# Seven block products in place of eight for the gate and up projections, with the block sums on VectorE

## Chip, core and metric

The kernel runs on one core of a Trainium2 chip. The metric is the device time of one execution in microseconds; lower is better. TensorE (PE; PEld are its weight loads) multiplies, VectorE (DVE) and ScalarE (ACT) do the elementwise work, SyncE (SP) issues the weight transfers from HBM. All arithmetic is f32.

## What is computed

Three transformer layers over 256 latent tokens (`x`) and 256 context tokens (`ctx`) of width 1024. Layer 0 has two kinds of attention and a feed-forward over both token sets, layer 1 has latent attention (MLA) and a feed-forward over the latent tokens alone, layer 2 has a gated linear recurrence, a gating unit and 16 experts. The change concerns the two feed-forwards (`ffn_w13` is 1024 x 5632, `ffn_w2` 2816 x 1024 per layer):

```python
def swiglu(h, w13, w2):
    gate, up = jnp.split(h @ w13, 2, axis=-1)
    return (jax.nn.silu(gate) * up) @ w2

# layer l, after attention (layer 0 does the same for ctx):
hx = modulate(rmsnorm(x, norm_g[l, 2]), mx[:, 3], mx[:, 4])
x = x + mx[:, 5] * rmsnorm(swiglu(hx, ffn_w13[l], ffn_w2[l]), norm_g[l, 3])
```

## The kernel before

Activations lie transposed in SBUF: `H[:, k, :]` holds channels 128k to 128k+127 of 512 tokens, the latent tokens in columns 0:256, the context in 256:512. A projection of 128 output columns is one accumulation over k = 0..7: stationary operand a 128x128 block of weights, moving operand `H[:, k, :]` (256 or 512 columns), output one of seven PSUM banks that are used in turn (`take`, `pe_dense`; L350 in `mm` issues every matmul).

Weights come through `ring`, six slots of 128x4096 f32 (2 MB), in the fixed order of `jobs`: job j goes to slot j % 6. SP issues them one after another and waits, before job j, until `weights_used` shows that job j-6 was read. A job `("w13", l, i)` holds 256 gate columns (0:256 of each k) and the 256 up columns that belong to them (256:512), so two pairs of 128; eleven such jobs, then eight jobs of `ffn_w2`.

First feed-forward (`pe_ffn0`, `act_ffn0`, `dve_ffn0`): the projections of jobs 0 and 1 run apart for the latent and the context half (256 columns each), because the context half is normalised later. Jobs 2 to 10, 18 pairs, run as gate and up with 512 columns: 16 matmuls a pair. ScalarE takes Silu of the gate product out of PSUM into `TG` (L935), VectorE multiplies by the up product into `HID` (L960) and so frees the bank. After the last of these, PE starts on `ffn_w2` with the same 512 tokens.

Second feed-forward (`pe_ffn1`, `act_ffn1`, `dve_ffn1`): the same over the 256 latent tokens, all 22 pairs alike, 16 matmuls of 256 columns each; Silu at L989, multiply at L998.

Every instruction of VectorE and ScalarE waits for the end of the one before on its own engine (`Chain.step`, `mark`, `free`); `full_of` waits for a PSUM bank to be full, `freed` for it to be empty again.

Of the kernel before, what the change touches and what calls it, by code (L numbers as in the profile page):

```python
# [23 lines left out]
P = 128  # L24
# [124 lines left out]
def build(nc, A, tab_f, tab_m, vrows, out):  # L149
    es = ExitStack()  # L150
    with es:
# [95 lines left out]
        logf_ready = Signal(sem("logf_ready"))  # L247


        jobs, job_at = [], {}  # L250

        def job(label, *dmas):
            job_at[label] = len(jobs)
            jobs.append(dmas)
# [37 lines left out]
        for i in range(2):  # L292
            job(("ab_out", i), rows(A["ab_w_out"][0], 0, D, i * 512, (i + 1) * 512))
        ffn_jobs(0)
# [34 lines left out]
        for j, dmas in enumerate(jobs):  # L329
            loads[j % SLOTS] += len(dmas)  # L330
            loaded_at.append(16 * loads[j % SLOTS])
# [26 lines left out]
        def weights(pe, label):  # L358
            j = job_at[label]
            pe.wait_ge(slot_loaded[j % SLOTS], loaded_at[j])  # L360
            return ring[:, j % SLOTS, :]
# [510 lines left out]

        HID = ar(0, KF, T2)
# [7 lines left out]
        def pe_ffn0(pe):  # L881
# [13 lines left out]
            for i in range(2, NW):  # L895
                w = w13(pe, 0, i)
                for j in range(2):
                    for g in range(2):
                        pe_dense(pe, ("gu"[g], 0, 2 * i + j), w, 256 * g + j * P, H, T2)
                used()  # L900
            freed(pe, ("u", 0, KF - 1))
# [14 lines left out]
        def act_ffn0(c):  # L916
# [15 lines left out]
            for j in range(4, KF):  # L932
                b = full_of(c.eng, ("g", 0, j))
                freed(c.eng, ("u", 0, j - 2) if j >= 6 else ("u", 0, j - 2, 1))
                c.free(S.activation(TG[:, j % 2, :], ps[:, b, :], ACT.Silu), ("g", 0, j))  # L935
# [13 lines left out]
        def dve_ffn0(c):  # L949
            for j in range(4):  # L950
# [4 lines left out]
            for j in range(KF):  # L955
                key, t = (("u", 0, j, 1), HALF[1]) if j < 4 else (("u", 0, j), slice(0, T2))
                freed(c.eng, ("g",) + key[1:])
                b = full_of(c.eng, key)
                src = ps[:, b, 0:TX] if j < 4 else ps[:, b, :]
                c.free(V.tensor_tensor(HID[:, j, t], TG[:, j % 2, t], src, ALU.mult), key)  # L960
# [10 lines left out]
        def pe_ffn1(pe):  # L971
            for i in range(NW):
# [5 lines left out]
            freed(pe, ("u", 1, KF - 1))  # L978
# [5 lines left out]
        def act_ffn1(c):  # L984
            for j in range(KF):
                b = full_of(c.eng, ("g", 1, j))
                if j >= 2:
                    freed(c.eng, ("u", 1, j - 2))
# [1312 lines left out]
```

## Time and profile before

| | |
|---|---|
| median of 3 runs | 2561.03 us (2557.65 to 2563.27) |
| the profiled execution | 2562.76 us |
| its span, first to last instruction | 2561.0 us |
| PE busy / PEld / DVE / ACT | 2096.5 / 1200.3 / 547.2 / 422.1 us |
| gate/up projections, first feed-forward (whole width) | from about 460 to 707 us |
| gate/up projections, second feed-forward | 1054.6 to 1210.4 us |
| experts | from about 1623 us to the end |

The page gives one profiled execution. An f32 matmul shows as two records of PE and two of PEld. The chain of waits names, from the end backwards, what each piece waited for; the share of an engine in it is the part of the time that it set.

### The profile page before, as it was taken

The numbers are of one execution on the slowest core, as the hardware profiler recorded it, in microseconds if no ns is written. First come the engines' busy times: TensorE is split into PE (matmuls) and PEld (weight loads), VectorE is DVE, ScalarE is ACT, GpSimd is POOL, SyncE is SP. The second block draws the span as 40 slices with busy tenths as digits, with TensorE's granted clock in tenths as the row PEclk, the third lists the DMA queues.
The fourth block names the chain that finished last, engine by engine and source line by source line (L and its number), as shares of the span: only waits on it lengthen the run. The fifth ranks groups of instructions, "written<-read, shape, count | busy, mean of one in ns | idle before, by whom it ended". The sixth has DMA issues, their size and how long they took to land.

```text
span 2561.0 us, 25876 instructions
## 1 busy us (share of the span) xinstructions
PE 2096.5 (82%) x10863; PEld 1200.3 (47%) x10863; DVE 547.2 (21%) x1203; ACT 422.1 (16%) x883; POOL 7.0 (0%) x15
## 2 busy tenths in 40 slices
PE   6998899999999999999999999755565656555555
PEld 3544368544446857888887777411111111111111
DVE  3217744000000456300026622200000000000001
ACT  3005534000000446300033221100000000000000
POOL 0000000000000000000000000000000000000000
PEclk9999999999999999999999989877778777778777
DMA  9447862221122440444532323699999999999996
GB/s 381 189 197 309 309 204 69 96 87 47 46 74 56 118 146 8 132 149 110 187 126 99 131 76 140 277 428 428 428 427 428 427 427 428 427 428 428 428 427 282
DMA packets 178498, 614.77 MB, mean 240 GB/s; under 512 B 26096, under 2 KB 119536, under 8 KB 144592
## 3 DMA queue, kind: packets, MB, share of 16 engines
q1 hardware_dynamic: 177568, 610.38, 60.9%
q0 software_dynamic: 816, 2.76, 0.4%
q8 instruction: 86, 1.41, 0.2%
q14 instruction: 28, 0.23, 0.0%
HBM read 612.06 MB, written 1.05 MB: 239 GB/s over the span
## 4 chain that ended last, share of the span: by engine, by line
PE 60%; DMA 33%; DVE 4%; ACT 1%; issue 1%; SPq 0%; DVEq 0%; ACTq 0%
PE ps L350 58%; DMA ring<-in_expert_w_up 13%; DMA ring<-in_expert_w_gate 11%; DMA ring<-in_expert_w_down 8%; DMA ring<-in_ab_w_in 1%; PE ps L762 1%; DVE ST L797 0%; DVE X L709 0%; DVE AR L708 0%; ACT AR L815 0%; ACT AR L827 0%; DVE H L660 0%; PE ps L491 0%; DVE AR L849 0%; PE ps L2019 0%
## 5 line engine op out<-in xcount | busy, mean ns | idle before, releaser
L350 PE MATMUL ps<-ring,AR 128*32 128x512 f32 (+1 forms) x4096 | 516.1, 651 | 359.8 <-DMA ring<-in_expert_w_up 128.9
L350 PE MATMUL ps<-H,ring 128*128 128x256 f32 (+1 forms) x2848 | 795.2, 441 | 8.2 <-ACT H L646 4.9
L350 PEld LDWEIGHTS ps<-H,ring 128*128 128x128 f32 x2848 | 542.8, 191 | 251.0 <-issue 193.2
L350 PEld LDWEIGHTS ps<-ring,AR 128*32 128x32 f32 x4096 | 143.0, 132 | 713.5 <-issue 241.2
L350 PE MATMUL ps<-AR,ring 128*128 128x256 f32 (+1 forms) x1228 | 316.7, 420 | 2.5 <-DVE AR L1788 1.0
L350 PEld LDWEIGHTS ps<-AR,ring 128*128 128x128 f32 x1228 | 234.6, 191 | 83.6 <-issue 53.1
L350 PE MATMUL ps<-AR 128*128 128x128 f32 (+5 forms) x848 | 129.9, 356 | 19.2 <-ACT AR L815 8.6
L2053 DVE TENSOR_TENSOR AR<-AR,ps 128x512 f32<-128x512 f32 x16 | 11.0, 687 | 581.1 <-PE ps L350 581.1
L350 PEld LDWEIGHTS ps<-AR 128*128 128x128 f32 (+2 forms) x848 | 88.4, 183 | 47.3 <-issue 38.4
L2039 ACT ACTIVATE AR<-ps 128x512 f32<-128x512 f32 x16 | 9.6, 597 | 535.5 <-PE ps L350 535.5
L2064 DVE TENSOR_TENSOR AR<-ps,X 32x256 f32<-32x256 f32 x64 | 26.9, 420 | 286.2 <-PE ps L350 284.5
L350 PE MATMUL ps<-ring,H 128*128 128x512 f32 (+1 forms) x224 | 76.6, 502 | 0.0
L350 PE MATMUL ps<-ring,SC 128*32 128x512 f32 x576 | 68.7, 602 | 2.5 <-DMA ring<-in_ada_w 2.5
L960 DVE TENSOR_TENSOR AR<-AR,ps 128x512 f32<-128x512 f32 (+1 forms) x22 | 14.1, 639 | 260.6 <-PE ps L350 260.6
L797 DVE TENSOR_REDUCE ST<-ps 128x1 f32<-128x512 f32 (+1 forms) x96 | 57.8, 602 | 25.9 <-PE ps L350 23.8
L815 ACT ACTIVATE AR<-ps,ST 128x512 f32<-128x512 f32 (+1 forms) x96 | 59.2, 617 | 24.1 <-DVE ST L804 20.9
L2045 ACT ACTIVATE AR<-ps 128x512 f32<-128x512 f32 x16 | 9.6, 597 | 319.3 <-PE ps L2019 319.3
L350 PEld LDWEIGHTS ps<-ring,H 128*128 128x128 f32 x224 | 37.5, 191 | 37.8 <-issue 37.7
L703 DVE TENSOR_TENSOR H<-H 128x256 f32<-128x256 f32 x21 | 8.9, 426 | 200.9 <-ACT H L689 200.8
L762 PEld LDWEIGHTS ps<-FTAB,AR 128*128 128x128 f32 x272 | 30.3, 143 | 42.7 <-issue 38.8
L762 PE MATMUL ps<-FTAB,AR 128*128 128x128 f32 x272 | 41.2, 284 | 10.3 <-DVE AR L849 7.2
L935 ACT ACTIVATE AR<-ps 128x512 f32<-128x512 f32 x18 | 10.8, 598 | 233.2 <-PE ps L350 233.2
(255 smaller groups left out, 1086.8 us busy)
## 6 DMA issues: line engine op xcount, KB each, us to landing
ring<-in_expert_w_gate SPq DMA_DIRECT2D x64, 2048.0 KB, 23.3
ring<-in_expert_w_up SPq DMA_DIRECT2D x64, 2048.0 KB, 23.3
ring<-in_expert_w_down SPq DMA_DIRECT2D x64, 2048.0 KB, 23.1
ring<-in_ada_w SPq DMA_DIRECT2D x36, 2048.0 KB, 10.1
ring<-in_ffn_w SPq DMA_DIRECT2D x44, 1024.0 KB, 7.6
ring<-in_w_in SPq DMA_DIRECT2D x12, 2048.0 KB, 7.9
ring<-in_ffn_w SPq DMA_DIRECT2D x16, 1408.0 KB, 7.1
ring<-in_ab_w_in SPq DMA_DIRECT2D x4, 2048.0 KB, 15.9
```

The lines of the kernel that those rows point to most:

```text
L350: m = nc.tensor.matmul(out_, lhsT=lhsT, rhs=rhs, start=start, stop=stop)
L703: ins = V.tensor_tensor(self.SQ(0)[:, self.t], self.SQ(0)[:, self.t], self.SQ(k)[:, self.t], ALU.add)
L762: m = nc.tensor.transpose(ps[:, b, j * P:(j + 1) * P], PR[:, i % 2, u, j * P:(j + 1) * P], ident)
L797: c.step(V.reduce_max(st[:, m:m + 1], ps[:, b, 0:g.nk], axis=AX_X))
L815: c.free(S.activation(PR[:, i % 2, m, 0:g.nk], ps[:, b, 0:g.nk], ACT.Exp, bias=st[:, 2 + m:3 + m], scale=g.scale, accum_out=st[:, 6 + m:7 ...
L935: c.free(S.activation(TG[:, j % 2, :], ps[:, b, :], ACT.Silu), ("g", 0, j))
L960: c.free(V.tensor_tensor(HID[:, j, t], TG[:, j % 2, t], src, ALU.mult), key)
L2039: c.free(S.activation(GT, ps[:, b, :], ACT.Silu), ("hg", e))
L2045: c.free(S.activation(HT.rearrange("p a b -> p (a b)"), ps[:, b, :], ACT.Copy), ("ht", e))
L2053: c.free(V.tensor_tensor(HS, GT, ps[:, b, :], ALU.mult), ("hu", e))
L2064: ins = V.tensor_tensor(YE[32 * q:32 * q + 32, g, t * TX:(t + 1) * TX], ps[32 * t:32 * t + 32, b, 0:TX], GFR[32 * t:32 * t + 32, t, :], AL ...
```

## The change

The product of each pair and all its tokens is seen as two by two blocks: the weights as gate and up (128 columns each) by lower and upper half of the 1024 channels, `A11, A12` (gate) and `A21, A22` (up); the activations as halves of the channels by halves of the tokens, `B11, B12, B21, B22` (first feed-forward: latent and context, 256 each; second: 128 and 128 latent tokens). Eight block products of four matmuls each become seven (Strassen's scheme in Winograd's form), with half as many columns per matmul: 28 matmuls of 256 columns in the first feed-forward in place of 16 of 512, 28 of 128 in the second in place of 16 of 256.

The new class `Pairs` has this work: `dve_four` makes the four sums of activations once per feed-forward; `dve_blocks` the four sums of weights for each pair (one of them in place, in the ring); PE runs the products 1, 2, 6, 7, 5, 4, 3; ScalarE copies product 1 out of PSUM and takes both Silus from SBUF; VectorE adds the other products together (seven adds) and does two multiplies by the Silus. PE waits for the block sums of a pair ahead of product 6. The sums of the next pair stand in VectorE's order after product 5.

Jobs 2 to 10 of the first feed-forward and 1 to 10 of the second are done so: 18 and 20 pairs. The four sums of activations of the first feed-forward lie in the ring slot of `ab_out` 1, which is kept until the last `w13` job was read; so each job now notes its own slot and the job that it has to wait for. The diff, with the parts that only rename left out:

```diff
@@ -245,12 +245,20 @@
         logf_ready = Signal(sem("logf_ready"))
         jobs, job_at = [], {}
+        slot_of, after, last_in = [], [], [s - SLOTS for s in range(SLOTS)]
         def job(label, *dmas):
-            job_at[label] = len(jobs)
+            s = min(range(SLOTS), key=lambda a: last_in[a])
+            slot_of.append(s)
+            after.append(int(last_in[s]))
+            last_in[s] = job_at[label] = len(jobs)
             jobs.append(dmas)
@@ -291,6 +299,8 @@
             job(("ab_out", i), rows(A["ab_w_out"][0], 0, D, i * 512, (i + 1) * 512))
+        held_slot = slot_of[job_at[("ab_out", 1)]]
+        last_in[held_slot] = len(jobs) + KF // 2 - 0.5
         ffn_jobs(0)
@@ -870,6 +880,120 @@
+        class Pairs:
+            def __init__(self, l, i0, T, H_, HID_, sums, four, C, V_, W):
+                self.l, self.T, self.HID, self.sums, self.four, self.C, self.V, self.W = l, T, HID_, sums, four, C, V_, W
+                self.at = [(i, j) for i in range(i0, NW) for j in range(2)]
+                self.x, self.y = slice(0, T), slice(T, 2 * T)
+                self.low, self.high = (H_[:, 4 * a:4 * a + 4, :] for a in range(2))
+                n = len(self.at)
+                self.four_base = four_ready.plan(1)
+                self.block_base = blocks_ready.plan(n)
+                self.silu = silu_ready.plan(2 * n)
+                self.hid = pair_hid.plan(2 * n)
+            def block(self, p, m, a):
+                i, j = self.at[p]
+                n = job_at[("w13", self.l, i)]
+                w = ring[:, slot_of[n], :].rearrange("p (k n) -> p k n", k=KD)
+                return w[:, 4 * a:4 * a + 4, 256 * m + j * P:256 * m + (j + 1) * P]
+            def pe(self, pe):
+                T1, T2, T3, T4 = self.four
+                (B11, _), (B21, B22) = ((h[:, :, self.x], h[:, :, self.y]) for h in (self.low, self.high))
+                for p, (i, j) in enumerate(self.at):
+                    if j == 0:
+                        w13(pe, self.l, i)
+                    S1, S2, S4 = self.sums[p % 2]
+                    A11, A12, S3, A22 = (self.block(p, m, a) for m in range(2) for a in range(2))
+                    for n, A_, B_ in ((1, A11, B11), (2, A12, B21), (6, S2, T2), (7, S3, T3), (5, S1, T1), (4, A22, T4),
+                                      (3, S4, B22)):
+                        b = take(pe, ("p", n, self.l, p))
+                        if n == 6:
+                            if p == 0:
+                                pe.wait_ge(four_ready.sem, self.four_base + 1)
+                            pe.wait_ge(blocks_ready.sem, self.block_base + p + 1)
+                        for k in range(4):
+                            mm(ps[:, b, 0:self.T], A_[:, k, :], B_[:, k, :], k == 0, k == 3, b if k == 3 else None)
+                    if j:
+                        used()
+            def act(self, c):
+                for p in range(len(self.at)):
+                    v, w = self.C[p % 2], self.V[p % 2]
+                    b = full_of(c.eng, ("p", 1, self.l, p))
+                    c.free(S.activation(v, ps[:, b, 0:self.T], ACT.Copy), ("p", 1, self.l, p))
+                    if p >= 2:
+                        c.eng.wait_ge(pair_hid.sem, self.hid + 2 * (p - 1))
+                    freed(c.eng, ("p", 2, self.l, p))
+                    c.mark(S.activation(TG[:, p % 2, self.x], v, ACT.Silu), silu_ready, self.silu + 2 * p + 1)
+                    freed(c.eng, ("p", 3, self.l, p))
+                    c.mark(S.activation(TG[:, p % 2, self.y], w, ACT.Silu), silu_ready, self.silu + 2 * p + 2)
+            def dve_four(self, c):
+                T1, T2, T3, T4 = self.four
+                (B11, B12), (B21, B22) = ((h[:, :, self.x], h[:, :, self.y]) for h in (self.low, self.high))
+                c.step(V.tensor_tensor(T1, B12, B11, ALU.subtract))
+                c.step(V.tensor_tensor(T2, B22, T1, ALU.subtract))
+                c.step(V.tensor_tensor(T3, B22, B12, ALU.subtract))
+                c.mark(V.tensor_tensor(T4, B21, T2, ALU.subtract), four_ready, self.four_base + 1)
+            def dve_blocks(self, c, p):
+                S1, S2, S4 = self.sums[p % 2]
+                A11, A12, A21, A22 = (self.block(p, m, a) for m in range(2) for a in range(2))
+                n = job_at[("w13", self.l, self.at[p][0])]
+                c.eng.wait_ge(slot_loaded[slot_of[n]], loaded_at[n])
+                c.step(V.tensor_tensor(S1, A21, A22, ALU.add))
+                c.step(V.tensor_tensor(A21, A11, A21, ALU.subtract))
+                c.step(V.tensor_tensor(S2, S1, A11, ALU.subtract))
+                c.mark(V.tensor_tensor(S4, A12, S2, ALU.subtract), blocks_ready, self.block_base + p + 1)
+            def hid_of(self, p, t):
+                i, j = self.at[p]
+                return self.HID[:, 2 * i + j, t]
+            def dve_gated(self, c, p, half, src):
+                c.eng.wait_ge(silu_ready.sem, self.silu + 2 * p + half + 1)
+                t = (self.x, self.y)[half]
+                c.mark(V.tensor_tensor(self.hid_of(p, t), src, TG[:, p % 2, t], ALU.mult), pair_hid,
+                       self.hid + 2 * p + half + 1)
+            def dve(self, c):
+                last = len(self.at) - 1
+                def product(p, n):
+                    return ps[:, full_of(c.eng, ("p", n, self.l, p)), 0:self.T]
+                self.dve_blocks(c, 0)
+                for p in range(last + 1):
+                    v, u, w = self.C[p % 2], self.V[p % 2], self.W
+                    y = self.hid_of(p, self.y)
+                    freed(c.eng, ("p", 1, self.l, p))
+                    p6 = product(p, 6)
+                    c.free(V.tensor_tensor(u, v, p6, ALU.add), ("p", 6, self.l, p))
+                    p2 = product(p, 2)
+                    c.free(V.tensor_tensor(v, v, p2, ALU.add), ("p", 2, self.l, p))
+                    if p:
+                        self.dve_gated(c, p - 1, 1, self.hid_of(p - 1, self.y))
+                    p7 = product(p, 7)
+                    c.free(V.tensor_tensor(w, u, p7, ALU.add), ("p", 7, self.l, p))
+                    p5 = product(p, 5)
+                    c.step(V.tensor_tensor(y, w, p5, ALU.add))
+                    c.free(V.tensor_tensor(u, u, p5, ALU.add), ("p", 5, self.l, p))
+                    if p < last:
+                        self.dve_blocks(c, p + 1)
+                    p4 = product(p, 4)
+                    c.free(V.tensor_tensor(w, w, p4, ALU.add), ("p", 4, self.l, p))
+                    self.dve_gated(c, p, 0, w)
+                    p3 = product(p, 3)
+                    c.free(V.tensor_tensor(u, u, p3, ALU.add), ("p", 3, self.l, p))
+                self.dve_gated(c, last, 1, self.hid_of(last, self.y))
         HID = ar(0, KF, T2)
@@ -892,13 +1016,8 @@
                     used()
-            for i in range(2, NW):
-                w = w13(pe, 0, i)
-                for j in range(2):
-                    for g in range(2):
-                        pe_dense(pe, ("gu"[g], 0, 2 * i + j), w, 256 * g + j * P, H, T2)
-                used()
-            freed(pe, ("u", 0, KF - 1))
+            pairs0.pe(pe)
+            pe.wait_ge(pair_hid.sem, pairs0.hid + 2 * len(pairs0.at))
@@ -929,10 +1048,9 @@
                     c.free(S.activation(TG[:, j % 2, HALF[part]], ps[:, b, 0:TX], ACT.Silu), ("g", 0, j, part))
-            for j in range(4, KF):
-                b = full_of(c.eng, ("g", 0, j))
-                freed(c.eng, ("u", 0, j - 2) if j >= 6 else ("u", 0, j - 2, 1))
-                c.free(S.activation(TG[:, j % 2, :], ps[:, b, :], ACT.Silu), ("g", 0, j))
+            for j in (2, 3):
+                freed(c.eng, ("u", 0, j, 1))
+            pairs0.act(c)
             smooth_table()
@@ -947,17 +1065,25 @@
         def dve_ffn0(c):
+            def first_hid(c, j):
+                key = ("u", 0, j, 1)
+                freed(c.eng, ("g",) + key[1:])
+                b = full_of(c.eng, key)
+                c.free(V.tensor_tensor(HID[:, j, HALF[1]], TG[:, j % 2, HALF[1]], ps[:, b, 0:TX], ALU.mult), key)
             for j in range(4):
...
                 c.mark(V.tensor_tensor(hid, hid, TG[:, j % 2, HALF[0]], ALU.mult), hid_ready, j + 1)
-            for j in range(KF):
-                key, t = (("u", 0, j, 1), HALF[1]) if j < 4 else (("u", 0, j), slice(0, T2))
-                freed(c.eng, ("g",) + key[1:])
-                b = full_of(c.eng, key)
-                src = ps[:, b, 0:TX] if j < 4 else ps[:, b, :]
-                c.free(V.tensor_tensor(HID[:, j, t], TG[:, j % 2, t], src, ALU.mult), key)
+            for j in range(2):
+                first_hid(c, j)
+            c.eng.wait_ge(weights_used, job_at[("ab_out", 1)] + 1)
+            for k in range(KD):
+                pre0f[1].ready(c.eng, k)
+            pairs0.dve_four(c)
+            for j in range(2, 4):
+                first_hid(c, j)
+            pairs0.dve(c)
             for k in range(1, SPLIT):
@@ -969,33 +1095,41 @@
         def pe_ffn1(pe):
-            for i in range(NW):
+            for i in range(1):
                 w = w13(pe, 1, i)
...
                 used()
-            freed(pe, ("u", 1, KF - 1))
+            pairs1.pe(pe)
+            pe.wait_ge(pair_hid.sem, pairs1.hid + 2 * len(pairs1.at))
+            for j in range(2):
+                freed(pe, ("u", 1, j))
             for n in range(KD):
...
         def act_ffn1(c):
-            for j in range(KF):
+            for j in range(2):
                 b = full_of(c.eng, ("g", 1, j))
-                if j >= 2:
-                    freed(c.eng, ("u", 1, j - 2))
                 c.free(S.activation(TG[:, j % 2, 0:TX], ps[:, b, 0:TX], ACT.Silu), ("g", 1, j))
+            for j in range(2):
+                freed(c.eng, ("u", 1, j))
+            pairs1.act(c)
             smooth_table()
...
         def dve_ffn1(c):
-            for j in range(KF):
+            for k in range(KD):
+                pre1f.ready(c.eng, k)
+            pairs1.dve_four(c)
+            for j in range(2):
                 freed(c.eng, ("g", 1, j))
...
                 c.free(V.tensor_tensor(HID1[:, j, :], TG[:, j % 2, 0:TX], ps[:, b, 0:TX], ALU.mult), ("u", 1, j))
+            pairs1.dve(c)
             for k in range(1, KD):
@@ -2102,6 +2236,13 @@
         yf = ar(11264, KD, T2)
+        def block_sums(at):
+            return [[ar(at + 1536 * q + 512 * a, 4, P) for a in range(3)] for q in range(2)]
+        pairs0 = Pairs(0, 2, TX, H, HID, block_sums(12288),
+                       [ring[:, held_slot, 1024 * a:1024 * (a + 1)].rearrange("p (k t) -> p k t", k=4) for a in range(4)],
+                       [RS[:, q * TX:(q + 1) * TX] for q in range(2)],
+                       [FREED[:, q * TX:(q + 1) * TX] for q in range(2)], FREED[:, 2 * TX:3 * TX])
         post0f = [PartPost(("ffn", 0), 0, 1, p, lambda k: yf[:, k, :], lambda k: H[:, k, :], SPLIT) for p in range(2)]
@@ -2111,6 +2252,8 @@
         yg = ar(5632, KD, TX)
+        pairs1 = Pairs(1, 1, P, H[:, :, HALF[0]], HID1, block_sums(8192), [ar(13312 + 512 * a, 4, P) for a in range(4)],
+                       [FREED[:, q * P:(q + 1) * P] for q in range(2)], [FREED[:, q * P:(q + 1) * P] for q in (2, 3)], FREED[:, 4 * P:5 * P])
         post1f = PartPost(("ffn", 1), 1, 1, 0, lambda k: yg[:, k, :], lambda k: H[:, k, :])
@@ -2179,11 +2322,11 @@
             for j, dmas in enumerate(jobs):
-                s = j % SLOTS
+                s = slot_of[j]
                 if j == 4:
                     sp.dma_start(FTAB[:, FT_FIRST:FT_W], tab_f[:, FT_FIRST:FT_W]).then_inc(tables_loaded, 16)
-                if j >= SLOTS:
-                    sp.wait_ge(weights_used, j - SLOTS + 1)
+                if after[j] >= 0:
+                    sp.wait_ge(weights_used, after[j] + 1)
                 for dst, src in dmas:
```

## Rows read from the trace of the kernel before

**Rows 1.** The page: slices of the span (GB/s), and the chain by engine, by line.

```profile
GB/s 381 189 197 309 309 204 69 96 87 47 46 74 56 118 146 8 132 149 110 187 126 99 131 76 140 277 428 428 428 427 428 427 427 428 427 428 428 428 427 282
...
PE 60%; DMA 33%; DVE 4%; ACT 1%; issue 1%; SPq 0%; DVEq 0%; ACTq 0%
```

**Rows 2.** Busy time by stretch: window and length, PE, PEld, DVE, ACT, POOL, clock, DMA, GB/s.

```profile
117.85:125.00 7.15, 7.15 (x66) 7.15 (x65) 4.03 (x7) 0.83 (x3) 0.00 (x0) 1.00 0.98 409
...
500.00:550.00 50.00, 50.00 (x118) 22.23 (x117) 2.75 (x4) 2.39 (x4) 0.00 (x0) 1.00 0.26 84
...
1100.00:1150.00 50.00, 50.00 (x233) 44.03 (x232) 2.95 (x7) 2.69 (x7) 0.00 (x0) 1.00 0.50 155
```

**Rows 3.** The waits of SP's queue: us in total, times, longest.

```profile
SPq L2188 <- PE ps L350: 2334.6, 287, 67.8
```

**Rows 4.** Timeline of DVE, first feed-forward: start, duration, instruction, idle time before it.

```profile
500.73 0.69 DVE L960 TENSOR_TENSOR AR<-AR,ps 128x512 f32<-128x512 f32 x1 [13.05 <-PE ps L350]
...
555.67 0.69 DVE L960 TENSOR_TENSOR AR<-AR,ps 128x512 f32<-128x512 f32 x1 [13.05 <-PE ps L350]
```

**Rows 5.** The same, where the first feed-forward has 256 columns (context half).

```profile
438.81 0.42 DVE L960 TENSOR_TENSOR AR<-AR,ps 128x256 f32<-128x256 f32 x1 [6.06 <-PE ps L350]
...
459.53 0.42 DVE L960 TENSOR_TENSOR AR<-AR,ps 128x256 f32<-128x256 f32 x1 [6.48 <-PE ps L350]
```

**Rows 6.** Timeline of ACT in the value projection of layer 0 (128 columns).

```profile
119.90 0.28 ACT L1062 ACTIVATE AR<-ps 128x128 f32<-128x128 f32 x1 [12.69 <-PE ps L350]
...
125.26 0.28 ACT L1062 ACTIVATE AR<-ps 128x128 f32<-128x128 f32 x1 [1.51 <-PE ps L350]
```

**Rows 7.** Groups of DVE by line and form: count, busy us, mean ns, idle before.

```profile
L1617 DVE TENSOR_TENSOR H<-AR 128x512 f32<-128x512 f32 x16 | 11.1, 692 | 0.5
...
L855 DVE COPY H<-ps 128x128 f32<-128x128 f32 x32 | 9.3, 292 | 6.9 <-PE ps L350 5.9
...
L1640 DVE TENSOR_TENSOR H<-AR 128x1024 f32<-128x1024 f32 x4 | 4.9, 1226 | 6.7 <-ACT AR L1600 6.7
```

**Rows 8.** Timeline of a normalisation, DVE and ACT in turn.

```profile
379.79 0.42 DVE L708 TENSOR_TENSOR AR<-AR,RS 128x256 f32<-128x256 f32 x1 [3.98 <-ACT RS L584]
380.24 0.42 DVE L709 TENSOR_TENSOR X<-X,AR 128x256 f32<-128x256 f32 x1
...
380.76 0.42 ACT L639 ACTIVATE H<-X 128x256 f32<-128x256 f32 x1 [1.06 <-DVE X L709]
...
393.52 0.42 ACT L584 ACTIVATE RS<-RS 128x256 f32<-128x256 f32 x1
394.05 4.13 DVE L666 SCALAR_TENSOR_TENSOR H<-X,AMP,RS 128x256 f32<-128x256 f32 x8 [3.62 <-ACT RS L584]
```

**Rows 9.** Groups of ACT by line and form.

```profile
L1062 ACT ACTIVATE AR<-ps 128x128 f32<-128x128 f32 x4 | 1.1, 278 | 17.2 <-PE ps L350 17.2
...
L639 ACT ACTIVATE H<-X 128x256 f32<-128x256 f32 x56 | 23.4, 417 | 33.4 <-DVE X L709 29.7 <-DVE X L565 2.8
...
L989 ACT ACTIVATE AR<-ps 128x256 f32<-128x256 f32 x22 | 8.4, 384 | 135.7 <-PE ps L350 135.7
```

**Rows 10.** Timeline where the second feed-forward goes over to ffn_w2.

```profile
1209.94 0.42 DVE L998 TENSOR_TENSOR AR<-AR,ps 128x256 f32<-128x256 f32 x1 [6.48 <-PE ps L350]
...
1210.41 4.80 PE L350 MATMUL ps<-AR,ring 128*128 128x256 f32 x21 [0.61 <-DVE AR L998]
```

**Rows 11.** The page's DMA issues: KB each, us to landing.

```profile
ring<-in_ffn_w SPq DMA_DIRECT2D x44, 1024.0 KB, 7.6
```

**Rows 12.** Groups by form: weight loads of the projections.

```profile
L350 PEld LDWEIGHTS ps<-H,ring 128*128 128x128 f32 x2816 | 537.6, 191 | 249.3 <-issue 193.2 <-ACT H L607 1.8 <-ACT H L646 1.0
```

**Rows 13.** Busy time and clock, columns as in rows 2.

```profile
280.00:300.00 20.00, 15.99 (x122) 7.04 (x122) 12.47 (x37) 10.80 (x29) 0.00 (x0) 1.00 0.79 300
...
1052.00:1056.00 4.00, 1.65 (x5) 1.00 (x4) 2.45 (x6) 2.81 (x7) 0.00 (x0) 0.73 0.00 0
```

More of the change, by code:

```diff
@@ L247, in build @@
         logf_ready = Signal(sem("logf_ready"))
+        four_ready = Signal(sem("four_ready"))
+        blocks_ready = Signal(sem("blocks_ready"))
+        silu_ready = Signal(sem("silu_ready"))
+        pair_hid = Signal(sem("pair_hid"))
         jobs, job_at = [], {}
+        slot_of, after, last_in = [], [], [s - SLOTS for s in range(SLOTS)]
         def job(label, *dmas):
-            job_at[label] = len(jobs)
+            s = min(range(SLOTS), key=lambda a: last_in[a])
+            slot_of.append(s)
+            after.append(int(last_in[s]))
+            last_in[s] = job_at[label] = len(jobs)
             jobs.append(dmas)
@@ L329, in build @@
         for j, dmas in enumerate(jobs):
-            loads[j % SLOTS] += len(dmas)
-            loaded_at.append(16 * loads[j % SLOTS])
+            loads[slot_of[j]] += len(dmas)
+            loaded_at.append(16 * loads[slot_of[j]])
         place, takes = {}, [0] * BANKS
@@ L359, in weights @@
             j = job_at[label]
-            pe.wait_ge(slot_loaded[j % SLOTS], loaded_at[j])
-            return ring[:, j % SLOTS, :]
+            pe.wait_ge(slot_loaded[slot_of[j]], loaded_at[j])
+            return ring[:, slot_of[j], :]
         def used():
```

## Prediction

> **What bounds the kernel now.** I read the page's chain of waits first, then the busy time by stage, then single stretches of the timeline. The chain is 60% TensorE and 33% DMA [rows 1]. The DMA part is the expert stage: from slice 26 on the transfers run at 427 to 428 GB/s [rows 1]. Both stretches that the change touches are TensorE's alone. In the first feed-forward's gate/up stage PE is busy 50.00 of 50 us at granted clock 1.00, DVE 2.75 and DMA 26%; in the second PE is again 50.00 of 50, DVE 2.95, DMA 50% [rows 2]. So TensorE time saved there shortens the path one for one, until another engine becomes late. The weight queue is no clock of its own: SP waited 2334.6 us for PE in 287 waits [rows 3]; slots are released by matmuls, so when PE is early the expert transfers start earlier by the same amount, with unchanged length.
>
> **TensorE's price of the products.** A pair (gate and up of 128 columns) is 16 matmuls of 512 columns in the first feed-forward. The same pass of VectorE over its result comes every (555.67 - 500.73)/4 = 13.735 us [rows 4]. At 256 columns, 16 matmuls take (459.53 - 438.81)/3 = 6.907 us [rows 5], 0.4317 each, in groups of eight with no extra per group. After the change a pair is 7 products of 4 matmuls: 28 x 0.4317 = 12.09 us. Saved: 1.65 us a pair, 18 pairs, **29.7 us**.
> In the second feed-forward a pair is 16 matmuls of 256 columns, 6.905 us; after it is 28 of 128 columns. The nearest row is the 32 matmuls of 128 columns in the value projection, shown as 64 records, two to a matmul, where ScalarE's evictions after each eight matmuls are (125.26 - 119.90)/3 = 1.787 us apart [rows 6]: 0.2233 each (a little more than half of 0.4317), so 28 x 0.2233 = 6.25 us. TensorE alone would save 0.65 x 20 = 13.1 us.
>
> **What VectorE gets.** Per pair: seven adds that read a product, two gate multiplies, four block sums of 128x512. Prices: 692 ns for 128x512 (also where, as in L1617, the operands are strided halves), 292 for 128x128, 1226 for 128x1024 [rows 7], 425 for 128x256 [rows 5, 8]; a dependent instruction follows about 0.03 us after the end of the one before, and a hand-over from VectorE to ScalarE or back costs 0.10 us [rows 8]. ScalarE: 0.38 to 0.42 at 256 columns; at 128 columns 0.278 from PSUM, and I estimate 0.31 from SBUF, by the same 0.03 that separate the two at 256 [rows 9]. PE's end to VectorE is 0.14 us, VectorE to PE 0.05 [rows 10].
> First feed-forward: 9 x 0.455 + 4 x 0.722 = 7.0 us a pair, with the one hop over ScalarE (0.10 + 0.42 + 0.03 + 0.38 + 0.10, less the gap counted) 8.0, against 12.09 of PE. It is covered with 4 us to spare. The new wait of PE for the sums sits before the third product; behind it in PE's queue are all later matmuls. The sums of the next pair are made after product 5 is read: 0.14 + 0.91 + 2.89 = 3.9 us against the four products (6.9 us) that PE has left. Free.
> Second feed-forward: here nothing is left over. The loop that VectorE and ScalarE must go round per pair, with no matmul in it: after the sums, add of product 4, gate multiply, add of product 3 (3 x 0.322 = 0.97); ScalarE's Silu of the second half and only behind it its copy of the next pair's product 1, since it takes them in that order (0.10 + 0.31 + 0.03 + 0.28 + 0.10, less 0.03, = 0.79); adds of 6 and 2, gate multiply, adds of 7 and twice 5 (6 x 0.322 = 1.93); four sums (2.89). Together **6.58, say 6.6 us**, against 6.25 of TensorE and 6.905 before. The loop through PE (sums ready, products 6, 7, 5, then adds and sums: 0.05 + 2.68 + 0.14 + 0.64 + 2.89 = 6.4) is a little shorter. So VectorE's chain sets the pace and PE idles 0.35 us in each pair: half of the saving there is lost.
>
> **The ends of the stages.** First feed-forward, start: VectorE must do four sums of 128x1024 (4 x 1.26 = 5.0 us) between the context products of columns 1 and 2, which come 6.9 us apart [rows 5]: hidden. The sums of pair 0 wait behind the last of these gate multiplies, 0.14 + 0.45 + 2.89 = 3.5 us after its matmuls, while PE has products 1 and 2 (3.45 us): 0.1 us. End: before, PE waited for one pass (0.14 + 0.69 + 0.05 = 0.88); now product 3, add, Silu, multiply: 0.14 + 0.42 + 0.10 + 0.42 + 0.10 + 0.42 + 0.05 = 1.65. So the first feed-forward gains 29.7 - 0.1 - 0.8 = **28.8 us**.
> Second: the first block (four projections as before) is unchanged, and the four sums of 128x512 made before its first eviction lie under its 13.8 us of matmuls. Then the sums of pair 0 end 3.5 us after its last matmul; 19 rounds of 6.6 follow; the last pair ends 5.8 us after its sums (four more products and the Silu tail, same prices). 3.5 + 125.4 + 5.8 = 134.7, against 20 x 6.905 + 0.61 [rows 10] = 138.7 before. **4.0 us** gained.
> The ring keeps one slot back for the four sums of the first feed-forward, so prefetch goes five deep in place of six. A two-part weight job lands in about 8 us [rows 11] and is used for 24.2; its cover is four jobs, some 97 us. Nothing on SP's queue comes later than it is needed. VectorE's own wait for the next job's weights is covered by the same lead; were it late, the adds of products 4 and 3 behind it would hold two PSUM banks that PE wants a pair later.
> Sum: 28.8 + 4.0 = 32.8. The profiled execution took 2562.8 us (span 2561.0), so 2530.0; the median of the runs shown is 1.7 lower, and I put the forecast at **2529**. All stages behind shift unchanged; re-warming of TensorE's clock at the gaps behind may move it by some 2 us.
>
> **Rivals.**
> A. ScalarE's hop or VectorE's small adds are cheaper and the second feed-forward is TensorE-bound: 19 x 0.35 = 6.6 us more, 2522. For it: only 0.35 us a pair separate the two. Against: every term comes from a row, and all VectorE instructions are dependent.
> B. The same chain is longer: instructions of 0.29 us with two or three waits each may follow less tightly than the 0.42 us ones of [rows 8], and a PE that restarts after a gap has to load weights first. At 7.1 us a pair the second feed-forward loses 5.5 us against before: 2539.
> C. Slower than before: the stationary loads bound the 128-column stream. In the value projection PEld was busy 7.15 of 7.15 us [rows 2], and a load shows 191 ns, two to a matmul, where 256 columns cover it [rows 12]. If long streams paid that in full, a matmul would take 0.382, a pair 28 x 0.382 = 10.7 us, 20 pairs 76 us more, and the whole 2563 - 28.8 + 76 = 2610. It decides from 6.905 + 28.8/20 = 8.3 us a pair, 0.298 per matmul. Against: those 32 matmuls ran at 0.2233 with a new load for each [rows 6].
> The Trainium skill, page "TensorE: Matmul & The Clock Gate", section "Back-to-back issue gap", speaks for C in a milder form: it gives about 81 ns for each load-and-matmul pair of 128 columns in a sustained stream. Taking our f32 matmul as four such passes that would be an estimate of 0.324, 9.07 us a pair, and 2577 in all. The row of 0.2233 disagrees, and I go by the row.
> D. The idle 0.35 us per pair lowers the granted clock. It fell to 0.73 where PE was busy only 1.65 of 4 us, but it stayed at 1.00 with 15.99 of 20 busy in many small gaps [rows 13]. At half clock a pair would need 12 us: about 2640. Little speaks for it.
> E. The gain is made and given back: a weight transfer becomes the late one behind. With the queue idle as in [rows 2, 3], I see no place; up to 2560.
>
> **How the numbers follow.** Forecast 0.60 (2525 to 2533), A 0.15, B 0.15 (up to 2545), C 0.04, D 0.02, E 0.04. A range from 2519 (A, less the 1.7 us and the clock's 2) to 2540 (B at 7.1 us) leaves out C, D, E and the end of B. About 0.2% (5 us) is what a measurement of this kernel can tell from no change. Faster by more: forecast, A, B and most of E, 0.93; within: 0.02; slower: C and D, with a little for what I don't see, 0.05.
>
> **What would show it.** Right: in the first feed-forward TensorE 100% busy at clock 1.00 and pairs 12.1 us apart, VectorE near 7 us of each; in the second, pairs 6.6 us apart, VectorE about 90% busy, PE waiting some 0.3 us a pair for the last block sum, loads all but continuous. The expert stage has its old length. Wrong: pairs at 6.25 (A) or above 6.9 (B) in the second, matmuls of 128 columns slower than 0.23 us while no wait is shown (C), a granted clock below 1.00 there (D), or waits of PE for in_ffn_w, mla or in2 transfers (E).

## Result and the profile after

The changed kernel takes 2530.04 us (median of 4 runs, 2527.80 to 2534.51) against 2561.35 before (median of 4, 2557.65 to 2563.27): a ratio of 0.9882, 95% interval 0.9870 to 0.9895, so 31.3 us less. The profiled execution took 2527.8 us, its span is 2525.8.

The page of the changed kernel: busy time, and the chain by engine, which answer to [rows 1].

```profile
PE 2053.2 (81%) x11775; PEld 1285.2 (51%) x11775; DVE 759.7 (30%) x1667; ACT 443.5 (18%) x959; POOL 7.0 (0%) x15
...
PE 57%; DMA 33%; DVE 7%; ACT 2%; issue 1%; SPq 0%; DVEq 0%; ACTq 0%
```

The chain is the chain of waits that ended last. PE's part of it fell from 60 to 57%, and DVE's rose from 4 to 7%: it now runs over VectorE somewhere. Busy time by stretch of the changed kernel (columns as in [rows 2]) says where:

```profile
500.00:550.00 50.00, 50.00 (x234) 44.01 (x233) 27.14 (x54) 5.29 (x13) 0.00 (x0) 1.00 0.27 85
1100.00:1150.00 50.00, 48.62 (x423) 47.49 (x423) 40.52 (x99) 6.60 (x22) 0.00 (x0) 1.00 0.40 112
```

In the first feed-forward PE is still busy all the time. In the second it is not, and VectorE is busy 40.52 of 50 us, at an unchanged clock of 1.00.

The span cut at the same five instructions in both traces (first matmul of the attention output; first of `ffn_w2`; first of the second feed-forward; first of its `ffn_w2`; first of the experts):

| stage, us | before | after | difference |
|---|---|---|---|
| up to the attention output | 347.00 | 344.73 | -2.27 |
| attention output, gate/up of the first feed-forward | 360.48 | 331.97 | **-28.51** |
| `ffn_w2` and MLA | 347.12 | 347.68 | +0.56 |
| gate/up of the second feed-forward | 155.81 | 153.33 | **-2.48** |
| rest up to the experts | 408.65 | 406.48 | -2.17 |
| experts | 941.94 | 941.61 | -0.33 |

The two changed stages give 31.0 of the 35.2 us by which the two profiled spans differ; the rest is stages that the change does not touch. Over the profiles of all kernels below, the first stage lies between 344.7 and 349.4 us and the one up to the experts between 406.5 and 409.2, while the 331.97 comes again to 0.01 us in each kernel that leaves that stage alone. A stage's length therefore tells more here than a median. The second feed-forward's is less steady: without any change to it one kernel below had 154.50 where the kernel before had 155.81. The difference lies in its first 32 matmuls, which are the same in all kernels but start at a granted clock of 0.50 for longer or shorter: until about 1060.3 us in the kernel before, 5.7 us into the stage, until about 1029 in the changed one, 4.6 us into it. So that stage is best cut in two, behind these 32 matmuls (busy time by stretch; the kernel before first, then the changed one):

```profile
1054.60:1071.50 16.90, 16.90 (x64) 14.18 (x65) 3.14 (x7) 5.88 (x11) 0.00 (x0) 0.82 0.40 125
1071.50:1210.41 138.91, 138.30 (x641) 121.41 (x639) 8.84 (x21) 8.96 (x21) 0.00 (x0) 1.00 0.43 128
```

```profile
1024.38:1040.59 16.21, 16.21 (x64) 13.71 (x65) 5.91 (x11) 5.88 (x11) 0.00 (x0) 0.86 0.40 129
1040.59:1177.71 137.12, 129.95 (x1122) 126.53 (x1120) 108.02 (x261) 18.41 (x61) 0.00 (x0) 1.00 0.44 130
```

Of the 2.48 us the change gives 138.91 - 137.12 = 1.8; the other 0.7 us is the clock at the stage's start (a mean of 0.86 in place of 0.82). The stretch of the changed pairs, from that cut to `ffn_w2`, is called the pair stretch below.

The first feed-forward after, timeline of VectorE: the same add of two successive pairs, to be held against [rows 4].

```profile
550.87 0.42 DVE L985 TENSOR_TENSOR AR<-FTAB,ps 128x256 f32<-128x256 f32 x1 [1.30 <-PE ps L360]
...
562.96 0.42 DVE L985 TENSOR_TENSOR AR<-FTAB,ps 128x256 f32<-128x256 f32 x1 [1.30 <-PE ps L360]
```

12.09 us apart, where it was 13.735. VectorE waits 1.30 us for PE here: it has room.

The second, as the chain of waits goes through one pair (start, length, what; the short pieces of "issue" between VectorE's instructions are left out):

```profile
1090.33 0.70 DVE AR L953
1091.04 0.14 issue
1091.17 2.93 PE ps L360 x24
1094.10 0.03 issue
1094.13 0.02 DVEq L379
1094.15 0.04 issue
1094.19 0.30 DVE AR L985
...
1094.52 0.30 DVE FTAB L986
...
1094.84 0.70 DVE AR L950
...
1095.57 0.70 DVE ring L951
...
1096.29 0.70 DVE AR L952
...
1097.02 0.70 DVE AR L953
1097.72 0.14 issue
1097.86 2.25 PE ps L360 x18
```

L953 is the last block sum. PE starts 0.14 us behind it, does products 6, 7 and 5 (24 records, 12 matmuls, 2.93 us), VectorE takes product 5 at 1094.19 in two adds and makes the four sums. From 1091.17 to 1097.86 are **6.69 us a pair**: less than the 6.905 of before, more than the 6.25 of TensorE alone. This is a loop through two engines: PE cannot start product 6 before VectorE's sums, and VectorE makes the next sums only behind product 5.

The four places where the stages begin and end, timeline of PE (in square brackets the idle time before):

```profile
460.74 1.53 PE L360 MATMUL ps<-ring,AR 128*128 128x256 f32 x6 [0.15 <-DVE AR L953]
...
676.70 1.55 PE L360 MATMUL ps<-AR,ring 128*128 128x512 f32 x3 [1.62 <-DVE AR L962]
...
1044.37 1.13 PE L360 MATMUL ps<-AR 128*128 128x128 f32 x8 [1.83 <-DVE AR L953]
...
1177.71 1.56 PE L360 MATMUL ps<-AR,ring 128*128 128x256 f32 x6 [1.25 <-DVE AR L962]
```

### The profile page after: what moved, and what is told of

The parts are those of the page before. It is cut to its first block, busy times and chain, and to the rows that moved or that the text cites. A ratio compares the mean times of both kernels' runs of the same rounds, so it can differ in the third digit from the quotient of the medians.

```text
span 2525.8 us, 28670 instructions
## 1 busy us (share of the span) xinstructions
PE 2053.2 (81%) x11775; PEld 1285.2 (51%) x11775; DVE 759.7 (30%) x1667; ACT 443.5 (18%) x959; POOL 7.0 (0%) x15
## 4 chain that ended last, share of the span: by engine, by line
PE 57%; DMA 33%; DVE 7%; ACT 2%; issue 1%; SPq 0%; DVEq 0%; ACTq 0%
PE ps L360 55%; DMA ring<-in_expert_w_up 14%; DMA ring<-in_expert_w_gate 9%; DMA ring<-in_expert_w_down 8%; PE ps L772 1%; DMA ring<-in_ada_w 1%; DVE AR L950 1%; DVE AR L953 1%; DVE AR L952 1%; DVE ring L951 1%; DVE ST L807 0%; DVE AR L718 0%; DVE X L719 0%; ACT AR L825 0%; ACT AR L837 0%
## 5 line engine op out<-in xcount | busy, mean ns | idle before, releaser
L360 PE MATMUL ps<-ring,AR 128*32 128x256 f32 (+2 forms) x4384 | 581.6, 631 | 360.6 <-DMA ring<-in_expert_w_up 133.5
L360 PEld LDWEIGHTS ps<-ring,AR 128*32 128x32 f32 (+1 forms) x4384 | 197.1, 135 | 719.5 <-issue 246.0
L360 PE MATMUL ps<-H,ring 128*128 128x256 f32 (+2 forms) x2240 | 513.5, 388 | 7.6 <-ACT H L656 5.1
L360 PEld LDWEIGHTS ps<-H,ring 128*128 128x128 f32 x2240 | 403.9, 192 | 103.8 <-issue 55.0
L360 PE MATMUL ps<-AR,ring 128*128 128x256 f32 (+2 forms) x1548 | 358.5, 389 | 3.9 <-DVE AR L962 2.9
L360 PEld LDWEIGHTS ps<-AR,ring 128*128 128x128 f32 x1548 | 273.3, 191 | 84.3 <-issue 53.1
L360 PE MATMUL ps<-AR 128*128 128x128 f32 (+5 forms) x1168 | 171.3, 332 | 25.2 <-ACT AR L825 8.6
L360 PE MATMUL ps<-ring 128*128 128x256 f32 x288 | 68.0, 379 | 0.0
L360 PE MATMUL ps<-H,AR 128*128 128x128 f32 (+2 forms) x320 | 60.5, 333 | 2.4 <-ACT H L617 2.4
L360 PEld LDWEIGHTS ps<-ring 128*128 128x128 f32 x288 | 54.7, 190 | 7.4
```

The source lines that it names most:

```text
L360: m = nc.tensor.matmul(out_, lhsT=lhsT, rhs=rhs, start=start, stop=stop)
```

## Experiments

**Which loop sets the second feed-forward.** The theory on record is VectorE's chain with ScalarE's hop: VectorE waits for ScalarE's copy of product 1, and ScalarE copies only behind a Silu that waits for VectorE. The trace after, where VectorE waits 0.09 us for product 5, speaks for the loop through PE. Two orders can be changed without changing any work.

`act_early`, ScalarE's copy of the next product 1 ahead of its second Silu (`copy` holds the two lines that stood at the head of the loop):

```diff
...
+                    if p + 1 < len(self.at):
+                        copy(p + 1)
                     freed(c.eng, ("p", 3, self.l, p))
                     c.mark(S.activation(TG[:, p % 2, self.y], w, ACT.Silu), silu_ready, self.silu + 2 * p + 2)
```

> ScalarE copies the next pair's product 1 before it takes the Silu of this pair's second half; nothing else moves. The changed kernel's pairs in the second feed-forward are 6.69 us apart. Theory on record (the chain of VectorE with ScalarE's hop in it sets the pace): the hop of 0.79 us leaves the chain, pairs come 6.4 us apart or less, 19 x 0.3 = 5.5 us or more gained. Rival, read off the trace after (the loop through the stopped PE sets it: sums ready, PE restarts 0.15 us later, three products 2.92, 0.10, two adds, four sums): pairs stay at 6.69 us, total within 1 us of the changed kernel, and VectorE's wait ahead of the add of product 5 grows from 0.1 us to some 0.9.

Timeline of VectorE and PE:

```profile
1091.51 0.29 DVE L990 TENSOR_TENSOR AR<-FTAB,ps 128x128 f32<-128x128 f32 x1 [0.49 <-PE ps L360]
...
1095.18 1.13 PE L360 MATMUL ps<-AR 128*128 128x128 f32 x8 [0.20 <-DVE AR L958]
...
1098.20 0.29 DVE L990 TENSOR_TENSOR AR<-FTAB,ps 128x128 f32<-128x128 f32 x1 [0.49 <-PE ps L360]
```

Pairs stay at 6.69 us. The hop is gone from VectorE's chain, and all that it bought is that VectorE waits longer for PE: 0.49 us for product 5, not the 0.9 expected there; another 0.44 comes ahead of the add of product 6. The time was 2533.85 us (0.9890, 0.9875 to 0.9905), nominally more than the changed kernel's; the pair stretch took 137.06 us (137.12 in the changed kernel), and the surplus lies in the first stage (349.4) and the one up to the experts (409.1).

`blocks_early`, the sums of the next pair ahead of the adds of product 5:

```diff
...
+                    if p < last:
+                        self.dve_blocks(c, p + 1)
                     p5 = product(p, 5)
                     c.step(V.tensor_tensor(y, w, p5, ALU.add))
                     c.free(V.tensor_tensor(u, u, p5, ALU.add), ("p", 5, self.l, p))
-                    if p < last:
-                        self.dve_blocks(c, p + 1)
```

> The four block sums of the next pair are made ahead of the two adds of product 5 and not behind them; ScalarE's order is as in the changed kernel. Loop through PE sets the pace: it gets 1.5 us shorter, and then the chain of VectorE with ScalarE's hop is what is left: pairs at 6.60 us, 19 x 0.09 = 1.7 us gained. Theory on record (that chain sets the pace already): it contains the same instructions in either order, so 6.69 us stays, 0 gained. If neither were a bound: 6.25.

Its timeline of VectorE: the first add behind the sums, and the add that waits for ScalarE's copy.

```profile
1092.14 0.29 DVE L987 TENSOR_TENSOR AR<-FTAB,ps 128x128 f32<-128x128 f32 x1
...
1094.53 0.29 DVE L977 TENSOR_TENSOR FTAB<-FTAB,ps 128x128 f32<-128x128 f32 x1 [0.80 <-ACT FTAB L928]
...
1098.74 0.29 DVE L987 TENSOR_TENSOR AR<-FTAB,ps 128x128 f32<-128x128 f32 x1
```

6.60 us: with the loop through PE shortened, the chain that the prediction had worked out is left, at its forecast length, with VectorE idle in it only for the hop. The median, 2530.00 (0.9874), shows no gain, but the trace does: the pair stretch took 134.12 us, 3.0 less. 1.7 of it are 19 x 0.09; the rest lies in the first pairs behind pair 0, where PE waits for no sums yet (three of them follow at 6.25 to 6.33 us).

`both_early`, the two together:

> Both moves. Each theory has both loops shorter than the products themselves: VectorE needs 9 x 0.322 + 4 x 0.722 = 5.8 us a pair. Then TensorE is the bound, 28 x 0.2233 = 6.25 us a pair, 19 x 0.44 = 8.4 us less than the changed kernel. If the 128-column matmul costs more in a long stream than in the 32 matmuls of the value projection (loads become the bound), pairs would be longer than 6.25 with PE never waiting.

2521.44 us (0.9843, 0.9828 to 0.9858), with a pair stretch of 128.53 us. Timeline of VectorE, the add of product 6:

```profile
1092.51 0.29 DVE L982 TENSOR_TENSOR FTAB<-FTAB,ps 128x128 f32<-128x128 f32 x1 [0.46 <-PE ps L360]
...
1098.77 0.29 DVE L982 TENSOR_TENSOR FTAB<-FTAB,ps 128x128 f32<-128x128 f32 x1 [0.46 <-PE ps L360]
```

The pairs are 6.26 us apart. In the pair stretch the two moves alone give 0.1 and 3.0 us, and neither shows in a median; together they give 8.6 us, in the pair stretch and in the median alike.

`all_early`, both moves, and the block sums of pair 0 one gate multiply earlier in both feed-forwards (shown for the second):

```diff
...
             for j in range(2):
+                if j:
+                    pairs1.dve_blocks(c, 0)
                 freed(c.eng, ("g", 1, j))
```

> As both_early, and the block sums of pair 0 ahead of the last gate multiply of the part before, in both feed-forwards. The changed kernel has PE idle 1.83 us there in the second and 0.15 us in the first. Expected: 1.9 us less than both_early, so some 10 us less than the changed kernel. If a bank or a transfer were late instead, no gain over both_early.

2519.00 us (2517.41 to 2519.35), ratio 0.9832 (0.9815 to 0.9848), the fastest of those that do no needless work; stages 331.58 and 142.41 us, 0.4 and 1.7 less than with both moves. Busy time by stretch:

```profile
1100.00:1150.00 50.00, 50.00 (x450) 50.00 (x449) 42.98 (x104) 7.17 (x24) 0.00 (x0) 1.00 0.44 117
```

PE and its loads are busy without a gap, at full clock.

**Each part alone.** `first_only` has the second feed-forward of before, `second_only` the first.

> Seven products in the first feed-forward alone; the second as in the kernel before. Prediction's sum: 28.8 us less than before (2532.5). By the traces of before and after the stage is 28.5 us shorter and nothing is given back, so 28 to 29 less. If the freed time were lost behind (a weight transfer late), less than 25.

> Seven products in the second feed-forward alone, first one and ring as before. Prediction's sum 4.0 us less than before; the trace after shows the stage 2.5 us shorter (pairs at 6.69 in place of 6.60). So 2.5 less, near the limit of what can be measured. If the parts act on each other, the two do not add up to 31.

`first_only` took 2532.90 us (0.9888, 0.9873 to 0.9902; 28.5 less than the 2561.4 beside it), stage 331.97: the first feed-forward is nearly everything. `second_only` took 2556.99 us (0.9985, 0.9976 to 0.9995; 4.4 less, with an interval of 1.3 to 6.1), pairs at 6.69 us: the second feed-forward is a small gain. Its trace puts it lower than the median does: 136.81 us for the pair stretch, 2.1 less than before. 28.5 and 4.4 add up to 32.9 against 31.3 measured together, within the intervals: no run shows the two acting on each other.

**What a block sum costs in the loop, and beside it.** The same sum made again, once a pair in the second feed-forward (below); four times, or three, with `self.l == 0` for the first:

```diff
...
+                if self.l == 1:
+                    for _ in range(1):
+                        c.step(V.tensor_tensor(S1, A21, A22, ALU.add))
                 c.step(V.tensor_tensor(S1, A21, A22, ALU.add))
```

> The changed kernel with one block sum per pair made twice, in the second feed-forward only (19 of them in the loop). If VectorE's instructions lie on the loop that sets the pace, each costs its whole 0.72 us: pairs at 7.41 us, total 14 us more. If PE set the pace and VectorE were only busy beside it, up to 0.44 us of it would be hidden.

2546.51 us, 16.5 more than the changed kernel. Timeline of VectorE, an add of product 5 in successive pairs:

```profile
1104.03 0.29 DVE L988 TENSOR_TENSOR AR<-FTAB,ps 128x128 f32<-128x128 f32 x1
...
1111.44 0.29 DVE L988 TENSOR_TENSOR AR<-FTAB,ps 128x128 f32<-128x128 f32 x1
```

Pairs are 7.41 us apart, 6.69 + 0.72: every sum costs its whole length there. The expected 14 us left out two things: the sum of pair 0 (0.7 us), and the clock behind the longer wait for it, seen in the timeline of PE and in busy time by stretch:

```profile
1047.38 1.61 PE L360 MATMUL ps<-AR 128*128 128x128 f32 x8 [2.55 <-DVE AR L956]
```

```profile
1047.40:1050.50 3.10, 3.10 (x17) 3.10 (x18) 0.58 (x2) 0.31 (x1) 0.00 (x0) 0.57 1.10 350
```

Pair 1 starts 9.04 us behind pair 0 there and not 7.41: 1.6 us more.

> The changed kernel with four more block sums per pair in the first feed-forward only (18 x 2.9 = 52 us more of VectorE work). Forecast: VectorE has 4 us to spare per pair and the sums 3.0 us ahead of their use, so the pairs stay 12.09 us apart and only pair 0 pays its 2.9 us (sums of pair 0 are not hidden): 3 us more in all. If VectorE shared a bound with PE there: up to 52 us.

This expectation failed: 2540.58 us, 10.5 more, and the stage was 341.22 us, 9.25 more. Timeline of PE, two starts of product 6 after a block sum:

```profile
567.11 1.97 PE L360 MATMUL ps<-ring,AR 128*128 128x256 f32 x8
...
579.47 1.97 PE L360 MATMUL ps<-ring,AR 128*128 128x256 f32 x8
```

12.36 us apart: a new bound, and by the same loop as in the second feed-forward. Twelve matmuls of 256 columns 5.18, two adds 0.91, eight sums 5.79; 0.48 is left for PE's stop, restart and hand-over. In the second feed-forward 6.69 - 2.68 - 0.65 - 2.89 = 0.47 is left. I had again allowed 0.14 on one side and nothing on the other. Of the 9.25 us, 17 x 0.27 = 4.6 are this, 2.9 the sums of pair 0, and the rest, 1.8, the clock behind their wait. Timeline of PE, and the granted clock (last but two):

```profile
466.55 2.98 PE L360 MATMUL ps<-ring,AR 128*128 128x256 f32 x8 [3.06 <-DVE AR L956]
...
469.32 2.60 PE L360 MATMUL ps<-ring 128*128 128x256 f32 x8
...
471.76 1.89 PE L360 MATMUL ps<-ring,AR 128*128 128x256 f32 x8
```

```profile
466.50:469.00 2.50, 2.45 (x8) 2.05 (x9) 0.00 (x0) 0.00 (x0) 0.00 (x0) 0.67 0.62 194
469.00:472.00 3.00, 3.00 (x12) 2.49 (x11) 0.84 (x2) 0.42 (x1) 0.00 (x0) 0.71 0.00 0
```

After 3.06 us of idleness two products took 5.21 us in place of 3.45: 0.67 and 0.71 are means of stretches at 1.00 and at 0.50, and by slices of 1 us the clock was 0.50 from 467.5 to 470.5. Two more runs test the loop:

> The changed kernel with three more block sums per pair in the first feed-forward (four gave 12.36 us a pair). If the loop sums, PE's restart, three products, two adds, sums sets that 12.36, one sum less gives 11.64, below the 12.09 of the products: pairs at 12.09 again, and only the sums of pair 0 cost their 2.2 us more, perhaps with a window of lower clock behind that wait. If VectorE's work slowed PE in proportion: 12.3.

> The version with everything early (sums of the next pair ahead of the adds of product 5, ScalarE's copy first, sums of pair 0 one multiply earlier), with the same four extra sums per pair in the first feed-forward that gave 12.36 us a pair. Loop theory: the loop now holds two products and one add, 12.36 - 1.73 - 0.46 = 10.2; VectorE needs 4.1 + 8 x 0.722 = 9.9. So the products bound: 12.09 a pair and no cost beyond pair 0's. If four extra sums cost by themselves (memory shared with PE): again 12.3 or more.

With three extra sums, timeline of PE (product 6 of two successive pairs):

```profile
572.20 1.89 PE L360 MATMUL ps<-ring,AR 128*128 128x256 f32 x8
...
584.28 1.89 PE L360 MATMUL ps<-ring,AR 128*128 128x256 f32 x8
```

12.08 us, and the stage is 2.18 us longer than the changed kernel's, its pair 0 alone; 2532.17 us. With four, but early, busy time by stretch:

```profile
500.00:550.00 50.00, 50.00 (x234) 44.01 (x233) 37.98 (x70) 4.86 (x12) 0.00 (x0) 1.00 0.27 84
```

VectorE is busy 76% of the time, PE is not slowed at all: stage 331.58 us, the same as without the extra sums, 2518.09 us in all. So it is the place of the sums in the order that costs, and neither VectorE's load nor a conflict of the two engines at the ring shows.

**The matmul of 128 columns in a long stream.** The kernel before, with its matmuls half as wide and twice as many, and no sums (shown for the second feed-forward):

```diff
...
+                        for h in range(2):
+                            for k in range(KD):
+                                mm(ps[:, b, h * P:(h + 1) * P], w[:, k, col:col + P], H[:, k, h * P:(h + 1) * P],
+                                   k == 0, k == KD - 1, b if k == KD - 1 and h else None)
```

> The kernel before with its eight block products kept, but each accumulation made in two halves of the tokens: the second feed-forward's jobs 1 to 10 in matmuls of 128 columns (32 a pair in place of 16), the first one's jobs 2 to 10 in matmuls of 256 (32 in place of 16 of 512). No block sums, VectorE and ScalarE as before. If the 128-column matmul costs its 0.2233 us in a long stream: 7.15 us a pair in place of 6.905, 20 x 0.24 = 4.9 us more in that stage; first stage 32 x 0.4317 = 13.81 in place of 13.735, 18 x 0.08 = 1.4 us more; together 6 us more than before. If the loads bound it at their 191 ns, two to a matmul: 12.2 us a pair, 106 us more. By the 0.324 that was estimated from the page: 10.4 us a pair, 69 us more.

2566.96 us (1.0023, 1.0013 to 1.0033): 5.9 more. Timeline of ScalarE and busy time by stretch:

```profile
1103.54 0.39 ACT L1002 ACTIVATE AR<-ps 128x256 f32<-128x256 f32 x1 [6.76 <-PE ps L350]
...
1110.69 0.39 ACT L1002 ACTIVATE AR<-ps 128x256 f32<-128x256 f32 x1 [6.76 <-PE ps L350]
```

```profile
1100.00:1150.00 50.00, 50.00 (x450) 50.00 (x450) 2.95 (x7) 2.69 (x7) 0.00 (x0) 1.00 0.50 156
```

7.15 us for 32 matmuls, 0.2234 each, for the whole stage, with the loads busy 50.00 of 50 us. The stages are 1.5 and 4.7 us longer. So in the second feed-forward halving the width costs 0.24 us a pair and leaving out the eighth product gives back 0.89.

The Trainium skill, page "TensorE: Matmul & The Clock Gate", section "Back-to-back issue gap", has 81 ns for a load and matmul of 128 columns in a stream, from which the prediction had an estimate of 0.324 us for our matmul. The stream of 0.2234 us above disagrees with that estimate. Whether the 81 ns or the taking of one f32 matmul as four such passes is at fault, no run here shows.

## Why the prediction was right, step by step

- **First feed-forward, forecast 28.8, measured 28.5 us.** The pair is 12.09 us as worked out from [rows 4, 5]. The end was 1.62 us of idleness (forecast 1.65), the start 0.15 (0.1). The missing 0.3 us lie in that start: `all_early`, where PE no longer stops there, has the stage 0.39 us shorter, so a stop that shows as 0.15 us costs 0.39. The cover that I named, VectorE's 4 us to spare, was there, but the margin of the block sums was smaller than I wrote: I set 3.9 us against four products, and left out that a loop through a stopped PE costs 0.48 us beside the products. With the change as it is this cost nothing; with four extra sums it decided.
- **Second feed-forward, forecast 4.0, measured 1.8 us**, less than half (2.5 with the 0.7 of the clock in its first 32 matmuls, which the change does not touch). A pair took 6.69 us, not 6.60: 19 x 0.09 = 1.7 us; one late pair (PE waits 0.54 us at 1158.38 in place of 0.20) and the end make up the rest. The failing step is "The loop through PE is a little shorter. So VectorE's chain sets the pace". Its terms 0.05 + 2.68 + 0.14 = 2.87 measured 0.14 + 2.93 + 0.09 = 3.16: PE's start behind VectorE is 0.14 and not the 0.05 that I took from [rows 10] (here the load starts 0.12 behind VectorE's end and the matmul 0.03 behind the load; why, no run isolates), and twelve matmuls from a standstill to the last one's end take 0.25 more than twelve in a stream. VectorE's chain was right (6.58 forecast, 6.60 with the loop through PE out of the way), and it was not the bound. That the two differ by only 0.09 us a pair is why the total hardly noticed. VectorE was 81% busy there and not 90: the 0.03 us between its instructions do not count as busy.
- **Start and end of that stage**: 1.83 us idle at pair 0 (forecast 3.5 - 1.8 = 1.7); the last pair ended 6.1 us behind its sums (forecast 5.8).
- **The rest shifts one for one**: experts 941.94 and 941.61 us. Nothing was given back (E), and PE waits for no weight transfer in either feed-forward, so the ring with one slot less was late nowhere.
- **Rivals.** A (second feed-forward bound by TensorE) is not what the change does, but what two moves in its order make of it, with a pair of 6.26 us against 6.25. B's 7.1 us did not occur, but one of its two reasons did, the PE that restarts: it is what makes 6.69 of 6.60, a fifth of B's way. Its other reason, looser VectorE instructions, did not: they start 0.32 us apart, as priced. C is refuted by the stream of 0.2234 us, D by the clock of 1.00 over the whole pair stretch, with its gaps of 0.20 us per pair.
- **The total** is right to 1 us partly by luck: the profiled execution was 2.2 us faster than its sum (2530.0), by stages that have nothing to do with the change, and the median is 2.2 us above it and not 1.7 below.

## What to carry to other kernels

Fewer products with narrower matmuls pay in full only if the adds stay out of TensorE's way: the second feed-forward got 1.8 us with them in the way and 12.4 with them out of it (138.91 before, 126.48 in `all_early`). Count not just each engine's work per round, but every loop through two engines; a stop and start of TensorE in it cost 0.47 to 0.48 us here. Where two loops have nearly the same length, shortening one shows little; a change of order that is worth 0.1 us alone can be worth 5.6 on top of another. Work for the next round belongs at the earliest place in an engine's order at which its inputs exist, not behind the results of this round.

## What the runs showed of the hardware that I had not expected

- A hand-over VectorE to PE to VectorE in a loop costs 0.47 us (6.69 us a pair, 128 columns) to 0.48 us (12.36, 256 columns) beyond the matmuls' rate in a stream. The idle time that the profile shows for PE is less: 0.20 us a pair, where the pair is 6.69 - 6.25 = 0.44 longer than TensorE's stream.
- An f32 matmul of 128 columns with a load of its own each time ran at 0.2234 us for a whole stage of 140 us, though a load shows 191 ns twice in [rows 12] and its row is busy 100% in the stream: the recorded length of a load is not its cost.
- VectorE at 76% busy, reading the ring slots that PE reads and writing one sum in eight back into them, did not slow PE by 0.01 us a pair (`four_sums_early`, 331.58 us as in `all_early`).
- After a wait of PE of 3.06 us the granted clock fell to 0.50, the lower of its two levels, for some 3 us (467.5 to 470.5, `extra_sums_1st`), and 1.8 us were lost; it fell about 1 us after PE had begun again. After one of 2.55 us in the second feed-forward (`extra_sum_2nd`, 0.50 from 1048.4 to 1051.0) 1.6 us were lost. After one of 2.33 us in the first (`three_sums_1st`) and one of 1.83 in the second (the changed kernel) it stayed at 1.00. Before each of the four PE had been busy at 1.00.
